# Seven block products in place of eight in the FFN input matrices, with the output matrices in depth parts

## The chip, the cores and the metric

The kernel runs on one core of a Trainium2 chip. The metric is its time on the device in microseconds (us). Engines are called PE (TensorE), DVE (VectorE), ACT (ScalarE), POOL (GpSimd) and SP (SyncE, which issues most DMAs here).

## What is computed

One step of a hybrid encoder of two layers, on 512 prompt tokens and 32 sample tokens with their caches, all in float32. The mixers (attention beside a gated recurrence in layer 0, a delta rule in layer 1) are not touched by the change. Around each mixer stand two half-step FFNs, four in all:

```python
def swiglu(h, w_in, w_out):
    gate, up = jnp.split(h @ w_in, 2, axis=-1)
    return (jax.nn.silu(gate) * up) @ w_out
...
for layer in range(DEPTH):
    x = x + 0.5 * swiglu(rms_norm(x, ffn1_norm[layer]), ffn1_w_in[layer], ffn1_w_out[layer])
    h = rms_norm(x, mix_norm[layer])
    ...
    x = x + o
    x = x + 0.5 * swiglu(rms_norm(x, ffn2_norm[layer]), ffn2_w_in[layer], ffn2_w_out[layer])
```

`w_in` is 1024 x 5632 (2816 gate columns, then 2816 up columns), `w_out` is 2816 x 1024.

## The kernel before

The 544 tokens lie along the free axis, the features on the 128 partitions, so `x` is 8 tiles of 128 x 544. A weight matrix is read in units of 1024 rows by 256 columns (1 MB): SP loads them alternately into `raw[0]` and `raw[1]`. Every operand is split into a rounded high half and the rest: ACT copies `raw` to `wh` (`split_hi`, L553), DVE subtracts to get `wl` (`split_lo`, L558), and PE adds three products, high by high, high by low, low by high (`mm3`, L573). The tokens go in two parts of 288 and 256 columns, so a unit is 8 depth tiles x 2 column tiles x 3 x 2 = 96 matmuls. The `x` side is split in the same way into `xh` and `xl`, the hidden layer into `hh` and `hl`.

An FFN first has 22 input units (`ffn_in_*`): a gate unit (s=0, PSUM slots 0 and 1) and an up unit (s=1, slots 2 and 3) for each of 11 pairs. DVE scales the gate by `rstd` (L714), ACT applies Silu (L677), POOL multiplies by `rstd` again (L698), DVE multiplies by the up part (L724), and ACT and DVE split the hidden tile (L685, L727). Then come 12 output units (`out_pe`, three depth parts for each of four column pairs); the parts of a column pair are added in PSUM, and DVE adds the two finished tiles to `x` (L818). 22 + 11 = 33 units' worth of matmuls in all, the last depth part being shorter.

The order on each engine is the order in which these functions are called; engines meet at semaphores. In the input phase most engines run a hardware loop over the pairs. ACT and DVE prepare the next unit's weights while PE works on the present one.

## Time and profile before

| | us |
|---|---|
| median of 3 runs | 2440.68 (2438.52 to 2443.16) |
| the profiled execution, its own time | 2437.53 |
| its span in the trace | 2435.7 |
| PE busy in the span | 2394.6 |
| DVE busy | 1091.7 |
| ACT busy | 786.6 |
| POOL busy | 375.9 |

The span is what the trace covers; the execution's own time is 1.8 us longer. "Busy" is the time in which an engine has at least one instruction under way. PE's matmuls overlap (one takes longer than the distance to the next), so their pace is read from a stretch and its count.

### The profile page before, as it was taken

The numbers are of one execution on the slowest core, as the hardware profiler recorded it, in microseconds if no ns is written. First come the engines' busy times: TensorE is split into PE (matmuls) and PEld (weight loads), VectorE is DVE, ScalarE is ACT, GpSimd is POOL, SyncE is SP. The second block draws the span as 40 slices with busy tenths as digits, with TensorE's granted clock in tenths as the row PEclk, the third lists the DMA queues.
The fourth block names the chain that finished last, engine by engine and source line by source line (L and its number), as shares of the span: only waits on it lengthen the run. The fifth ranks groups of instructions, "written<-read, shape, count | busy, mean of one in ns | idle before, by whom it ended". The sixth has DMA issues, their size and how long they took to land.

```text
span 2435.7 us, 45344 instructions
## 1 busy us (share of the span) xinstructions
PE 2394.6 (98%) x19160; PEld 2344.4 (96%) x19160; DVE 1091.7 (45%) x1405; ACT 786.6 (32%) x1006; POOL 375.9 (15%) x324
## 2 busy tenths in 40 slices
PE   7999999999999999999999999999999999999998
PEld 7999999988989999999999999999999899999998
DVE  5333332556574333322433332488655654333322
ACT  4333322333323222222322222345345543222222
POOL 2101000000142111000111100143033531011000
PEclk9999999999999999999999999999999999999999
DMA  3223223322202222222222222323200012222221
GB/s 127 91 86 99 82 79 103 101 89 83 68 21 93 87 86 86 82 96 84 95 94 86 86 78 96 98 70 87 71 29 1 10 44 87 87 95 92 83 92 54
DMA packets 191213, 193.66 MB, mean 80 GB/s; under 512 B 4811, under 2 KB 188495, under 8 KB 191082
## 3 DMA queue, kind: packets, MB, share of 16 engines
q1 hardware_dynamic: 178286, 181.64, 23.1%
q10 hardware_dynamic: 12162, 8.11, 1.2%
q0 software_dynamic: 640, 2.10, 0.3%
q8 instruction: 97, 1.59, 0.3%
q14 instruction: 28, 0.22, 0.0%
HBM read 185.73 MB, written 6.10 MB: 79 GB/s over the span
## 4 chain that ended last, share of the span: by engine, by line
PE 94%; DVE 4%; issue 1%; ACT 1%; POOL 0%; DMA 0%; ACTq 0%; DVEq 0%
PE ps L573 81%; PE ps L2522 1%; PE ps L2507 1%; PE ps L2653 1%; DVE wl L558 1%; PE ps L2495 1%; PE ps L1092 0%; PE ps L1560 0%; PE ps L1657 0%; PE ps L780 0%; PE ps L2547 0%; PE ps L2541 0%; PE ps L2553 0%; PE ps L2562 0%; PE ps L1708 0%
## 5 line engine op out<-in xcount | busy, mean ns | idle before, releaser
L573 PE MATMUL ps<-xh,wh 128*128 128x288 f32 x3776 | 780.6, 288 | 3.6 <-DVE wl L558 2.8
L573 PE MATMUL ps<-xl,wh 128*128 128x288 f32 x3776 | 778.4, 287 | 0.0
L573 PE MATMUL ps<-xh,wl 128*128 128x288 f32 x3776 | 775.3, 287 | 0.0
L558 DVE TENSOR_TENSOR wl<-raw,wh 128x2048 fp32r<-128x2048 f32 (+1 forms) x173 | 390.7, 2258 | 505.0 <-ACT wh L553 505.0
L573 PEld LDWEIGHTS ps<-xh,wh 128*128 128x128 f32 x3776 | 577.4, 188 | 16.2 <-issue 8.0
L573 PEld LDWEIGHTS ps<-xh,wl 128*128 128x128 f32 x3776 | 578.1, 188 | 0.0
L573 PEld LDWEIGHTS ps<-xl,wh 128*128 128x128 f32 x3776 | 576.2, 188 | 0.0
L553 ACT ACTIVATE wh<-raw 128x2048 fp32r<-128x2048 f32 (+1 forms) x173 | 323.3, 1869 | 324.7 <-PE ps L573 318.8
L573 PE MATMUL ps<-hl,wh 128*128 128x288 f32 (+1 forms) x1408 | 289.9, 287 | 0.0
L573 PE MATMUL ps<-hh,wl 128*128 128x288 f32 (+1 forms) x1408 | 288.7, 286 | 0.0
L573 PE MATMUL ps<-hh,wh 128*128 128x288 f32 (+1 forms) x1408 | 286.7, 285 | 0.0
L698 POOL TENSOR_TENSOR gbuf<-gbuf,rstd 128x544 f32<-128x544 f32 x88 | 119.9, 1365 | 880.7 <-ACT gbuf L677 880.7
L573 PEld LDWEIGHTS ps<-hh,wl 128*128 128x128 f32 x1408 | 215.3, 188 | 0.0
L573 PEld LDWEIGHTS ps<-hh,wh 128*128 128x128 f32 x1408 | 215.0, 188 | 0.0
L573 PEld LDWEIGHTS ps<-hl,wh 128*128 128x128 f32 x1408 | 214.4, 188 | 0.0
L685 ACT ACTIVATE hh<-sq 128x544 f32 (+1 forms) x88 | 58.1, 660 | 389.2 <-DVE sq L724 389.2
L724 DVE TENSOR_TENSOR sq<-ps,gbuf 128x544 f32<-128x544 f32 x88 | 63.7, 724 | 244.0 <-PE ps L573 244.0
L714 DVE TENSOR_TENSOR gbuf<-ps,rstd 128x544 f32<-128x544 f32 x88 | 63.6, 723 | 201.7 <-PE ps L573 200.3
L677 ACT ACTIVATE gbuf<-gbuf 128x544 f32<-128x544 f32 x88 | 57.5, 658 | 283.4 <-DVE gbuf L714 283.2
L610 POOL TENSOR_TENSOR ssq<-ssq,sq 128x544 f32<-128x544 f32 x49 | 69.4, 1416 | 433.1 <-ACT sq L592 432.2
L818 DVE SCALAR_TENSOR_TENSOR x<-ps,x 128x544 f32 (+1 forms) x48 | 34.6, 723 | 111.7 <-PE ps L573 99.3
L589 ACT ACTIVATE xh<-x,cols (+1 forms) x48 | 36.0, 750 | 141.8 <-DVE x L818 128.7
(430 smaller groups left out, 2191.5 us busy)
## 6 DMA issues: line engine op xcount, KB each, us to landing
raw<-ffn_w_in SPq DMA_DIRECT2D x88, 1024.0 KB, 5.1
raw<-ffn_w_out SPq DMA_DIRECT2D x32, 1024.0 KB, 5.1
raw<-odd_w_in SPq DMA_DIRECT2D x16, 1024.0 KB, 5.6
raw<-even_w_in SPq DMA_DIRECT2D x14, 1024.0 KB, 5.0
raw<-ffn_w_out SPq DMA_DIRECT2D x16, 768.0 KB, 4.9
raw<-even_w_out SPq DMA_DIRECT2D x4, 1024.0 KB, 5.3
raw<-odd_w_out SPq DMA_DIRECT2D x4, 1024.0 KB, 5.4
xnat<-x_prompt SPq DMA_DIRECT2D x2, 1024.0 KB, 8.5
```

Of the source, the lines that this page charges most:

```text
L553: nc.scalar.activation(wh[slot][:, 0:kt, :], raw[slot][:, 0:kt, :], ACT.Copy).then_inc(hi_done.sem, 1)
L558: nc.vector.tensor_tensor(wl[slot][:, 0:kt, :], raw[slot][:, 0:kt, :], wh[slot][:, 0:kt, :].bitcast(F32), ALU.subtract).then_inc(lo_done.s ...
L573: ins = nc.tensor.matmul(ps[:, 2 * pe_out + b, PCOLS[b]], w, r[:, rk, TOKENS[b]], start=first and a == 0, stop=last and a == 2)
L589: nc.scalar.activation(tile(xh, m), tile(x, m), ACT.Copy, scale=gain_of(n, m)).then_inc(xh_ready.sem, 1)
L610: nc.gpsimd.tensor_tensor(ssq[:], ssq[:], sq[m % 2][:], ALU.add).then_inc(ssq_done.sem, 1)
L677: nc.scalar.activation(gbuf[c][:], gbuf[c][:], ACT.Silu).then_inc(gate_silu.sem, 1)
L685: nc.scalar.activation(tile(hh, 2 * j + c), sq[c][:], ACT.Copy).then_inc(hh_ready.sem, 1)
L698: nc.gpsimd.tensor_tensor(gbuf[c][:], gbuf[c][:], rstd[:], ALU.mult).then_inc(gate_rstd.sem, 1)
L714: nc.vector.tensor_tensor(two(gbuf[c][:]), halves(c), two(rstd[:]), ALU.mult).then_inc(gate_scaled.sem, 1)
L724: nc.vector.tensor_tensor(two(sq[c][:]), halves(2 + c), two(gbuf[c][:]), ALU.mult).then_inc(h_made.sem, 1)
L818: nc.vector.scalar_tensor_tensor(out=two(tile(x, m)), in0=halves(2 * q + c), scalar=scale, in1=two(tile(x, m)), op0=ALU.mult, op1=ALU.add) ...
L2495: ins = nc.tensor.transpose(bank(g, 2, n, n)[:, h, :], dX[g][0:n, h, 0:n], ident[0:n, 0:n])
```

## The change

The 22 input units of each FFN become one whole unit as before, three "plain" units whose weights are split in four blocks of 512 elements a partition, and 18 "seven" units. A seven unit cuts its 1024 x 256 weights into 2 x 2 blocks (depth halves by column tiles) and the activations into 2 x 2 blocks (depth halves by token halves of 272), and makes 7 block products by Strassen's scheme (Winograd's form) in place of 8. For it POOL makes four sums of weight blocks for every seven unit (`weight_sums`), and DVE, once for each FFN, the normed activations (`bop_normed`), their four sums (`token_sum`) and, with ACT, their halves (`bop`, seven blocks). The products are put together from PSUM by DVE (`u2c`, `u3c` and four results), with one copy by ACT (`m1c`). High and low halves of weight blocks lie in a ring of eight entries of 512 elements (`entry`).

The functions that go (`ffn_in_*`) are printed above. PE's part of a seven unit, and its waits:

```diff
+        for i, o in enumerate(S_ORDER):
+            op = u.op + i
+            pe.wait_ge(op_lo.sem, op_lo.at(op + 1))
+            if u.at == 2 * LEAD_PAIRS:
+                pe.wait_ge(bop_lo.sem, bop_lo.at(7 * f + i + 1))
+            if i == 4:
+                pe.wait_ge(m1_copied.sem, m1_copied.at(u.seven + 1))
+            if i == 5:
+                pe.wait_ge(block_out.sem, block_out.at(outs_before[u.seven] + 1))
+            if i == 6:
+                pe.wait_ge(block_out.sem, block_out.at(outs_before[u.seven] + 3))
+            w_hi, w_lo = entry(op)
+            for k in range(KH):
+                for a, (w, r) in enumerate(((w_hi, 7 + o), (w_hi, o), (w_lo, 7 + o))):
+                    ins = nc.tensor.matmul(ps[:, bank + S_BANK[i], 0:TH], w[:, k, :], bop[:, r, k, :],
+                                           start=i in S_OPEN and k == 0 and a == 0,
+                                           stop=k == KH - 1 and a == 2, skip_group_check=i in S_ADDED)
+            ins.then_inc(op_used.sem, 1)
```

The sources of the seven weight blocks, their splits, and the sums on POOL:

```diff
+    def op_source(u, i):
+
+        if u.kind != "seven":
+            return block_raw(u, *PLAIN_BLOCKS[i], block_nk(u, i))
+        if i in (0, 4, 5):
+            return block_raw(u, *{0: (0, 0), 4: (0, 1), 5: (1, 1)}[i])
+        return sums_of(u)[:, {2: 0, 1: 1, 3: 2, 6: 3}[i], :, :]
...
+    def op_split_lo(dve, u, i):
+        op, nk = u.op + i, block_nk(u, i)
+        hi, lo = entry(op)
+        dve.wait_ge(op_hi.sem, op_hi.at(op + 1))
+        nc.vector.tensor_tensor(lo[:, 0:nk, :], op_source(u, i), hi[:, 0:nk, :].bitcast(F32), ALU.subtract).then_inc(op_lo.sem, 1)
...
+    def weight_sums(pool, u):
+
+        s, slot, out = u.seven, u.raw % 2, sums_of(u)
+        first = u.seven - ffns[u.f][2 * LEAD_PAIRS].seven
+        pool.wait_ge(raw_loaded[slot].sem, raw_loaded[slot].at(8 * (u.raw - slot) + 16))
+        if first in (2, 3):
+            pool.wait_ge(op_used.sem, op_used.at(ffns[u.f][2 * LEAD_PAIRS].op))
+        elif first > 3:
+            back = [v for v in ffns[u.f] if v.kind == "seven" and v.seven == s - 2][0]
+            pool.wait_ge(op_lo.sem, op_lo.at(back.op + 7))
+        nc.gpsimd.tensor_tensor(out[:, 0, :, :], block_raw(u, 1, 0), block_raw(u, 1, 1), ALU.add).then_inc(sum_made.sem, 1)
+        pool.wait_ge(sum_made.sem, sum_made.at(4 * s + 1))
+        nc.gpsimd.tensor_tensor(out[:, 1, :, :], out[:, 0, :, :], block_raw(u, 0, 0), ALU.subtract).then_inc(sum_made.sem, 1)
+        nc.gpsimd.tensor_tensor(out[:, 2, :, :], block_raw(u, 0, 0), block_raw(u, 1, 0), ALU.subtract).then_inc(sum_made.sem, 1)
+        pool.wait_ge(sum_made.sem, sum_made.at(4 * s + 2))
+        nc.gpsimd.tensor_tensor(out[:, 3, :, :], block_raw(u, 0, 1), out[:, 1, :, :], ALU.subtract).then_inc(sum_made.sem, 1)
```

DVE's part. `next_split` makes a split for the next unit; before an output unit there are only four, at places 3 to 6:

```diff
+    def tail_dve(dve, u):
+
+        if u.kind != "seven":
+            return
+        into = gbuf if u.s == 0 else sq
+        dve.wait_ge(op_used.sem, op_used.at(u.op + 7))
+        nc.vector.tensor_tensor(into[0][:, TH:T], u2c[:], ps[:, 4 * u.s + 2, 0:TH], ALU.add).then_inc(block_out.sem, 1)
+        if u.s == 1:
+            dve.wait_ge(block_silu.sem, block_silu.at(3 * (u.seven // 2) + 3))
+            dve.wait_ge(block_out.sem, block_out.at(outs_before[u.seven] + 6))
+            nc.vector.tensor_tensor(sq[0][:, TH:T], sq[0][:, TH:T], gbuf[0][:, TH:T], ALU.mult).then_inc(h_made.sem, 1)
+            hidden_lo(dve, u, 1, 1)
+
+    def late_tail_dve(dve, u):
+
+        if u.kind == "seven" and u.s == 1:
+            hidden_lo(dve, u, 0, 2)
+
+    def ffn_seven_dve(dve, u):
+        before, pair, outs = ffns[u.f][u.at - 1], u.seven // 2, outs_before[u.seven]
+        into = gbuf if u.s == 0 else sq
+        bank = lambda i: ps[:, 4 * u.s + i, 0:TH]
+        tail_dve(dve, before)
+        next_split(dve, op_split_lo, u, 0)
+        late_tail_dve(dve, before)
+        next_split(dve, op_split_lo, u, 1)
+        dve.wait_ge(m1_copied.sem, m1_copied.at(u.seven + 1))
+        dve.wait_ge(op_used.sem, op_used.at(u.op + 2))
+        nc.vector.tensor_tensor(u2c[:], m1c[:], bank(1), ALU.add).then_inc(block_out.sem, 1)
+        next_split(dve, op_split_lo, u, 2)
+        next_split(dve, op_split_lo, u, 3)
+        dve.wait_ge(block_out.sem, block_out.at(outs + 1))
+        dve.wait_ge(op_used.sem, op_used.at(u.op + 4))
+        nc.vector.tensor_tensor(u3c[:], u2c[:], bank(3), ALU.add).then_inc(block_out.sem, 1)
+        dve.wait_ge(block_out.sem, block_out.at(outs + 2))
+        nc.vector.tensor_tensor(into[1][:, TH:T], u3c[:], bank(2), ALU.add).then_inc(block_out.sem, 1)
+        next_split(dve, op_split_lo, u, 4)
+        if u.s == 1:
+            dve.wait_ge(block_silu.sem, block_silu.at(3 * pair + 1))
+            dve.wait_ge(op_used.sem, op_used.at(u.op + 5))
+            nc.vector.tensor_tensor(sq[0][:, 0:TH], bank(0), gbuf[0][:, 0:TH], ALU.mult).then_inc(block_out.sem, 1)
+        next_split(dve, op_split_lo, u, 5)
+        dve.wait_ge(op_used.sem, op_used.at(u.op + 6))
+        nc.vector.tensor_tensor(into[1][:, 0:TH], u3c[:], bank(1), ALU.add).then_inc(block_out.sem, 1)
+        next_split(dve, op_split_lo, u, 6)
+        if u.s == 1:
+            dve.wait_ge(block_silu.sem, block_silu.at(3 * pair + 2))
+            dve.wait_ge(block_out.sem, block_out.at(outs + 5))
+            nc.vector.tensor_tensor(sq[1][:], sq[1][:], gbuf[1][:], ALU.mult).then_inc(h_made.sem, 1)
```

The activations' part on DVE ahead of the first seven unit, and the raw slots on SP:

```diff
+    def bop_normed(dve, f, n, k):
+
+        first = 6 if k < KH else 4
+        nc.vector.scalar_tensor_tensor(out=bopf[:, first:first + 2, k % KH, :], in0=two(x[:, k, :]), scalar=gain(n, k),
+                                       in1=two(rstd[:]), op0=ALU.mult, op1=ALU.mult).then_inc(bop_norm.sem, 1)
...
+        def token_sum(out, a, b, done, needs):
+            dve.wait_ge(bop_norm.sem, bop_norm.at(8 * f + done))
+            if needs:
+                dve.wait_ge(bop_sum.sem, bop_sum.at(4 * f + needs))
+            nc.vector.tensor_tensor(bopf[:, out, :, :], bopf[:, a, :, :], bopf[:, b, :, :], ALU.subtract).then_inc(bop_sum.sem, 1)
...
+        for k in range(KH):
+            bop_normed(dve, f, n, k)
+        op_split_lo(dve, units[2], 0)
+        token_sum(3, 7, 6, 4, 0)
+        op_split_lo(dve, units[2], 1)
+        for k in range(KH, KT):
+            bop_normed(dve, f, n, k)
+        op_split_lo(dve, units[2], 2)
+        token_sum(1, 5, 7, 8, 0)
+        token_sum(2, 5, 3, 8, 1)
+        op_split_lo(dve, units[2], 3)
+        token_sum(0, 4, 2, 8, 3)
+        hidden(0, 0)
+        hidden(0, 1)
+        hidden_lo(dve, units[1], 0, 1)
+        hidden_lo(dve, units[1], 1, 2)
+        for i in range(4):
+            op_split_lo(dve, units[3], i)
         if f == 0:
             lam_dve(dve)
...
+        gate(1, 0)
+        for i in range(4):
+            bop_split_lo(dve, f, i)
+        gate(1, 1)
+        op_split_lo(dve, units[4], 0)
+        bop_split_lo(dve, f, 4)
+        op_split_lo(dve, units[4], 1)
+        bop_split_lo(dve, f, 5)
+        hidden(1, 0)
+        op_split_lo(dve, units[4], 2)
+        bop_split_lo(dve, f, 6)
+        for i in (3, 4, 5, 6):
+            op_split_lo(dve, units[4], i)
+        hidden(1, 1)
+        hidden_lo(dve, units[3], 0, 1)
+        hidden_lo(dve, units[3], 1, 2)
...
+    def raw_free(sp, index):
+
+        if index < 2:
+            return
+        if index - 2 in plain_of:
+            sp.wait_ge(lo_done.sem, lo_done.at(plain_of[index - 2] + 1))
+            return
+        u = by_raw[index - 2]
+        if u.kind == "seven":
+            sp.wait_ge(sum_made.sem, sum_made.at(4 * u.seven + 4))
+            sp.wait_ge(op_lo.sem, op_lo.at(u.op + 6))
         else:
-            with dve.Fori(0, 2) as jj:
```

The output matrix now comes in three parts, each after the input pairs that make its depth (pairs 0 to 3, 4 to 7, 8 to 10), so that `hh` and `hl` hold 8 tiles in place of 22; DVE adds each part to `x` by itself:

```diff
+            m = 2 * q + c
+            dve.wait_ge(op_used.sem, op_used.at(u.op + 2 * c + 2))
+            if p:
+                dve.wait_ge(x_part.sem, x_part.at(16 * f + 8 * (p - 1) + m + 1))
+            nc.vector.scalar_tensor_tensor(out=two(x[:, m, :]), in0=halves(2 * u.s + c), scalar=0.5, in1=two(x[:, m, :]),
+                                           op0=ALU.mult, op1=ALU.add).then_inc((x_part if p < 2 else x_ready).sem, 1)
+            if c == 0 and v and v.kind == "seven":
+                for i in range(4, 7):
+                    op_split_lo(dve, v, i)
```

The loops are written out. The seven units of an FFN stand in groups of two, four and three pairs, between the lead (units 0 to 3) and the output units.

Where the instructions stand. DVE, one pair of the input phase before (the body of its loop; `wl` and `wh` are the halves of the weights, `gbuf` the gate, `sq` the hidden tile, `hl` its low half):

```order
L558 TENSOR_TENSOR wl1_50<-raw1,wh1_49 128x2048
...
L714 TENSOR_TENSOR gbuf0_66<-ps,rstd 128x544
...
L714 TENSOR_TENSOR gbuf1_67<-ps,rstd 128x544
...
L558 TENSOR_TENSOR wl0<-raw0,wh0 128x2048
...
L724 TENSOR_TENSOR sq0<-ps,gbuf0_66 128x544
...
L724 TENSOR_TENSOR sq1<-ps,gbuf1_67 128x544
...
L727 TENSOR_TENSOR hl_65<-sq0,hh_64 128x544
...
L727 TENSOR_TENSOR hl_65<-sq1,hh_64 128x544
```

DVE after the change, inside the second group of the first FFN, first the gate unit (with the tail of the up unit before it), then the up unit:

```order
L1119 TENSOR_TENSOR sq0<-u2c_75,ps 128x272
L1123 TENSOR_TENSOR sq0<-sq0,gbuf0_68 128x272
L887 TENSOR_TENSOR hl_65<-sq1,hh_64 128x544
L766 TENSOR_TENSOR wl1_50<-raw1,wh1_49 128x512
L887 TENSOR_TENSOR hl_65<-sq0,hh_64 128x544
L766 TENSOR_TENSOR wl0<-wsum1_73,wh0 128x512
L1141 TENSOR_TENSOR u2c_75<-m1c_74,ps 128x272
L766 TENSOR_TENSOR wl0<-wsum1_73,wh0 128x512 x2
L1146 TENSOR_TENSOR u3c_76<-u2c_75,ps 128x272
L1148 TENSOR_TENSOR gbuf1_69<-u3c_76,ps 128x272
L766 TENSOR_TENSOR wl0<-raw1,wh0 128x512
L766 TENSOR_TENSOR wl1_50<-raw1,wh1_49 128x512
```

```order
L1119 TENSOR_TENSOR gbuf0_68<-u2c_75,ps 128x272
L766 TENSOR_TENSOR wl1_50<-raw0,wh1_49 128x512
L766 TENSOR_TENSOR wl1_50<-wsum0_72,wh1_49 128x512
L1141 TENSOR_TENSOR u2c_75<-m1c_74,ps 128x272
L766 TENSOR_TENSOR wl0<-wsum0_72,wh0 128x512 x2
L1146 TENSOR_TENSOR u3c_76<-u2c_75,ps 128x272
L1148 TENSOR_TENSOR sq1<-u3c_76,ps 128x272
L766 TENSOR_TENSOR wl0<-raw0,wh0 128x512
L1153 TENSOR_TENSOR sq0<-ps,gbuf0_68 128x272
L766 TENSOR_TENSOR wl0<-raw0,wh0 128x512
L1156 TENSOR_TENSOR sq1<-u3c_76,ps 128x272
```

One subtraction of 2048 elements a unit has become seven of 512, and between them stand five additions of 272 with one operand in `ps`; the product `sq` by `gbuf` of 544 and one of 272 now have both operands in SBUF, and hidden low halves stand among the splits.

POOL before (the loop over the pairs and its end; `ssq` belongs to the next norm), and after:

```order
L698 TENSOR_TENSOR gbuf0_66<-gbuf0_66,rstd 128x544
...
L698 TENSOR_TENSOR gbuf1_67<-gbuf1_67,rstd 128x544
...
L694 COMPARE_AND_BRANCH
L606 COPY ssq_52<-sq0 128x544
```

```order
L954 TENSOR_TENSOR gbuf0_68<-gbuf0_68,rstd 128x544
L954 TENSOR_TENSOR gbuf1_69<-gbuf1_69,rstd 128x544
L972 TENSOR_TENSOR wsum_first0_70<-raw0 128x512
L974 TENSOR_TENSOR wsum_first0_70<-wsum_first0_70,raw0 128x512
L975 TENSOR_TENSOR wsum_first0_70<-raw0 128x512
L977 TENSOR_TENSOR wsum_first0_70<-raw0,wsum_first0_70 128x512
L954 TENSOR_TENSOR gbuf0_68<-gbuf0_68,rstd 128x544
L954 TENSOR_TENSOR gbuf1_69<-gbuf1_69,rstd 128x544
```

Behind the two gate products that each pair had, POOL now has four sums of 512 elements for each seven unit, all with both inputs in SBUF.

DVE in the lead of the first FFN after the change (`bopf` are the normed activations and their sums); before, a single split and the two products of the pair stood here:

```order
L909 SCALAR_TENSOR_TENSOR bopf_67<-x,cols,rstd 128x2x272 x4
L766 TENSOR_TENSOR wl0<-raw0,wh0 128x512
L1006 TENSOR_TENSOR bopf_67<-bopf_67 128x1088
L766 TENSOR_TENSOR wl0<-raw0,wh0 128x512
L909 SCALAR_TENSOR_TENSOR bopf_67<-x,cols,rstd 128x2x272 x4
L766 TENSOR_TENSOR wl0<-raw0,wh0 128x512
L1006 TENSOR_TENSOR bopf_67<-bopf_67 128x1088 x2
L766 TENSOR_TENSOR wl0<-raw0,wh0 128x512
L1006 TENSOR_TENSOR bopf_67<-bopf_67 128x1088
L1000 TENSOR_TENSOR sq0<-ps,gbuf0_68 128x544
```

The last of these rows is the FFN's first hidden product; all the others stand ahead of it.

## Rows read from the trace of the kernel before

**Rows 1.** The page: busy shares of the engines, chain by engine.
```profile
PE 2394.6 (98%) x19160; PEld 2344.4 (96%) x19160; DVE 1091.7 (45%) x1405; ACT 786.6 (32%) x1006; POOL 375.9 (15%) x324
...
PE 94%; DVE 4%; issue 1%; ACT 1%; POOL 0%; DMA 0%; ACTq 0%; DVEq 0%
```

**Rows 2.** The chain in order of time, layer 1's first FFN: start, us, what.
```profile
1166.75 392.49 PE ps L573 x3168
```

**Rows 3.** Stages: one stretch of an FFN, columns as its head says.
```profile
core 0: us, PE busy (x) PEld busy (x) DVE busy (x) ACT busy (x) POOL busy (x), PEclk, DMA share, GB/s
810.00:1040.00 230.00, 230.00 (x1859) 230.00 (x1858) 83.94 (x76) 59.60 (x57) 24.52 (x18) 1.00 0.28 90
```

**Rows 4.** The chain again, output matrix after layer 1's mixer.
```profile
1977.80 6.39 PE ps L2653 x48
...
1985.07 12.12 PE ps L2653 x96
```

**Rows 5.** Groups by form, DVE: busy us, mean ns, idle before.
```profile
L558 DVE TENSOR_TENSOR wl<-raw,wh 128x2048 fp32r<-128x2048 f32 x157 | 362.6, 2309 | 389.0 <-ACT wh L553 389.0
...
L727 DVE TENSOR_TENSOR hl<-sq,hh 128x544 f32 x80 | 57.6, 720 | 15.9 <-ACT hh L685 15.9
...
L596 DVE SCALAR_TENSOR_TENSOR xl<-x,cols,xh x32 | 25.0, 781 | 9.1 <-ACT xh L589 9.1
...
L625 DVE RECIPROCAL rstd<-ssq 128x544 f32<-128x544 f32 x6 | 21.3, 3550 | 8.8 <-ACT ssq L621 8.8
```

**Rows 6.** DVE in order of time in an FFN unit: start, us, instruction.
```profile
910.24 0.72 DVE L724 TENSOR_TENSOR sq<-ps,gbuf 128x544 f32<-128x544 f32 x1 [5.22 <-PE ps L573]
910.88 0.71 DVE L727 TENSOR_TENSOR hl<-sq,hh 128x544 f32 x1
```

**Rows 7.** DVE in order of time, layer 1's mixer, 256 elements.
```profile
1794.00 0.43 DVE L2229 TENSOR_TENSOR s<-ps,s 128x256 f32<-128x256 f32 x1 [0.20 <-PE ps L2084]
1794.34 0.41 DVE L2230 TENSOR_TENSOR s<-ps,s 128x256 f32<-128x256 f32 x1
```

**Rows 8.** DVE in order of time, layer 1's mixer, 512 elements, and POOL then.
```profile
1780.37 0.69 DVE L2396 TENSOR_TENSOR dBl<-dBT,dlev 128x512 f32<-128x512 f32 x1
...
1781.70 1.26 DVE L2396 TENSOR_TENSOR dBl<-dBT,dlev 128x512 f32<-128x512 f32 x1
...
1781.14 1.27 POOL L2365 TENSOR_TENSOR dU<-ident,dBl 128x512 f32<-128x512 f32 x1 [5.86 <-DVE dBl L2396]
```

**Rows 9.** DVE in order of time, layer 1's mixer, beside rows 10.
```profile
1894.84 1.28 DVE L2435 TENSOR_TENSOR dW<-ps,dW 128x512 f32<-128x512 f32 x2
...
1899.68 3.35 DVE L2009 TENSOR_TENSOR db<-db,ort 128x512 f32<-128x512 f32 x2
```

**Rows 10.** POOL in order of time, the same stretch.
```profile
1894.64 1.27 POOL L2373 TENSOR_TENSOR db<-db,egam 128x512 f32<-128x512 f32 x1
...
1898.33 5.83 POOL L2357 TENSOR_TENSOR dBl<-dBT,dlev 128x512 f32<-128x512 f32 x4
```

**Rows 11.** Groups by form, ACT.
```profile
L685 ACT ACTIVATE hh<-sq 128x544 f32 x80 | 52.8, 660 | 358.5 <-DVE sq L724 358.5
...
L2315 ACT ACTIVATE dZ<-ps 128x512 f32<-128x512 f32 x40 | 23.9, 597 | 13.8 <-PE ps L2507 6.9 <-PE ps L2541 6.9
```

**Rows 12.** DMA issues, the last number is us to landing.
```profile
raw<-ffn_w_in SPq DMA_DIRECT2D x88, 1024.0 KB, 5.1
```

**Rows 13.** The page's group of POOL's gate products.
```profile
L698 POOL TENSOR_TENSOR gbuf<-gbuf,rstd 128x544 f32<-128x544 f32 x88 | 119.9, 1365 | 880.7 <-ACT gbuf L677 880.7
```

**Rows 14.** Stages around PE's longest pause inside the kernel, and its waits.
```profile
719.60:723.00 3.40, 0.69 (x8) 0.45 (x5) 3.21 (x6) 2.04 (x4) 0.00 (x0) 1.00 0.00 0
723.00:726.40 3.40, 3.40 (x14) 3.40 (x15) 2.39 (x3) 1.82 (x2) 0.00 (x0) 0.50 0.00 0
...
PE ps L780 <- DVE mixl L1500: 2.7, 1, 2.7
...
PE ps L1560 <- DVE hq L1465: 1.3, 1, 1.3
```

609 lines of the change are left out of this document (429 added, 180 removed).

## The prediction

> **What bounds the kernel now.** I read the page's shares, then the chain that ended last, then the stages. PE is busy 98% of the span and the chain is 94% PE [rows 1]. Inside an FFN the chain is one unbroken piece of 3168 matmuls, 392.49 us, in each of the four [rows 2]: 3168/96 = 33 units, so 11.893 us a unit and 123.9 ns a matmul. Nothing ever makes PE wait there, while DVE is busy 36% of that time, ACT 26%, POOL 11% [rows 3]. Fewer matmuls therefore shorten the kernel until another engine becomes the bound; DVE is the candidate.
>
> **What is removed.** Of the 22 input units of an FFN, four stay (one whole, three in blocks) and 18 become seven products of 4 x 3 matmuls: 84 of 272 columns in place of 96 of 288 and 256. At 123.9 ns a unit falls to 10.41 us, at most 72 x 1.49 = 107 us in all. But an FFN unit sends two matmuls through each stationary block before the operand pair changes; a product changes it after every one, hi, hi, lo. The output matrix after layer 1's mixer already runs so: 48 matmuls of 288 columns took 6.39 us (133.1 ns), the next 96, half of each width, 12.12 us, 126.3 ns at a mean of 272 [rows 4]. I take that: a product is 1.515 us, a seven unit 10.61 us, saving 1.287 x 72 = **92.7 us**. The 48 output units keep their matmuls. The sum is made against the profiled execution: 2437.5 us, span 2435.7, and 3.2 below the median of the three runs.
>
> **What DVE gets.** A low-half split of 512 elements replaces a quarter of one of 2048. A 512-element operation with two SBUF inputs takes 0.69 us undisturbed [rows 8], 544 takes 0.72 [rows 5]; back to back, operations start 0.08 us earlier than the last one ends (544: 0.64 apart, 256 from PSUM: 0.34 apart) [rows 6, 7]. So I charge 0.61 for a split, 0.64 for 544 elements, 0.35 for a PSUM addition of 272, 0.13 more where it needs the one before.
> - Gate unit (s=0): first the tail of the up unit before it, addition 0.48, product 0.42, two hidden low halves 1.28; then u2, u3 and two results, 1.53, between 7 splits, 4.27. The first split waits 0.7 us, since ACT makes the hidden high half (0.66) and then that split's high half (about 0.6) only after the product [rows 11]. 8.7 us.
> - Up unit (s=1): the gate unit's last addition 0.43, u2 to the results 1.53, two products 0.35+0.66, splits 4.27, and 1.5 us waiting for Silu, two high halves and the M1 copy on ACT. 8.7 us.
>
> That is 17.4 us a pair of units against PE's 21.2. The ends for what the trace doesn't show: an addition of 272 costs between 0.34 (256) and 0.64 (544), ten of them a pair; I stay at the near end. ACT comes to about 6.3 us a unit from its rows, no bound.
>
> **What POOL gets, and what that does to DVE.** POOL now makes four sums of 512 elements for each seven unit, 1.27 us each [rows 10]: 5 us of 10.6. The trace shows what happens beside DVE. With one operand in PSUM nothing: two L2435 operations beside running POOL work took 1.28 together [rows 9]. With both in SBUF DVE stood still: L2396 took 0.69 alone and 1.26 when a POOL operation had begun before it [rows 8]; two L2009 took 3.35, 1.68 each, beside POOL's four L2357, which took 5.83 instead of four times 1.27 [rows 9, 10]. They alternate, and each POOL operation costs DVE 1.68-0.61 = 1.07 us. Splits, bop low halves, hidden low halves and two of the products all have both inputs in SBUF.
>
> The Trainium skill ("SBUF — State Buffer", section "Who interferes with whom") speaks against the change here: such a pair of instructions excludes each other for the whole instruction. The row agrees, save that it charges 1.07 us; by the page's whole 1.27, eight sums would cost a pair up to 10.1 us instead of 8.6, some 1 us more a pair after what hides, 24 us over the 24 pairs that have a burst.
>
> The sums come in a burst. Raw slot v+2 is free after split 5 of unit v, its DMA lands 5.1 us later [rows 12], then POOL starts. I laid a pair out, DVE and POOL alternating. Gate unit: the burst begins 2 to 4 us in, at the first splits; with a sum under u2 (0.35) or under u3 and its result (0.83), of 4.3 us between 3.1 and 3.6 are added, 3.6 once the bursts have moved forward. Up unit: the burst begins near split 3; u3 with its result (0.83), the bank 0 product (0.35) and the last result (0.35) hide 1.5, and 2.8 are added. A pair then takes DVE 12.3+11.55 = **23.85 us**. That is above PE's 21.2, and no better than the 23.79 that the pair costs today. PE loses 2.65 us a pair: product 5 waits for u2, product 6 for the result behind u3 (the banks are reused).
>
> Not every pair pays. Units before output units have no burst beside them (output matrices need no sums) and the last one only four splits, so the last pair of each group runs at PE's pace. DVE may also fall behind by 1.5 to 2 us before product 6 notices: in a free run the result behind u3 is ready 6.9 us into a unit and needed at 9.1. Groups of 4, 3 and 2 pairs: three bursts, 3 x 2.65-1.5 = 6.4; two bursts, 2 x 2.65-1.5 = 3.8; the group of 2 follows the lead.
>
> **The lead**, units 0 to 3, is 4 x 11.9 = 48 us of PE, and the two matmuls of the norm's statistics. DVE must add 8 normed tiles (two SBUF inputs, 0.78 [rows 5]), 4 token sums and 7 low halves of 1088 elements (1.2 to 1.3 each, on the line from 720 ns for 544 to 2309 for 2048): 6+5+9 = 20 us, beside 19 splits (11.6), 8 gate and product operations (5.2), 4 hidden low halves (2.6) and the reciprocal 3.55 [rows 5]. That is 43 us; it starts about 9 us in, behind the statistics, and POOL's four gate products (1.36 each [rows 13]) and first four sums block some 6 us more. So DVE is through with `ffn_lead_dve` near 58 us, the first seven unit starts at 49. Its products 3 and 4 wait about 2 us for their split, then product 5 waits for u2, queued behind the lead: I charge **8 us** an FFN for lead and first group (from 3, if POOL's work falls into DVE's waits, to 14).
>
> Output units: DVE adds each depth part to x, 8 x 0.64 us twice more an FFN, with 4 splits in 11.9 us: hidden under PE. The last hidden tile is ready about 2.4 us after the last product and is needed after 24 matmuls, 2.97 us: nothing. Unrolled loops: nothing.
>
> **Clock.** After a pause of 2.71 us of PE the granted clock was 0.50 for 3.4 us, in which 14 matmuls went in place of 28 [rows 14]. The wait behind each lead is of that size: 1.7 us, 4 times 7 us. The pauses of 1 to 1.6 us in the pairs I charge nothing: one of 1.3 us left the clock alone.
>
> **Sum:** 2437.5-92.7+4 x (6.4+3.8+8)+7 = 2437.5-92.7+72.8+7 = 2424.6, with 3.2 for the median **2428 us**, 0.5% faster. What a measurement tells from no change is 0.2%, 4.9 us.
>
> **Rivals.**
> - *POOL's sums hide* (0.27): bursts mostly fall under PSUM additions, DVE's waits for ACT or for PE. For it: a DVE pair is 17.4 us, and 6.5 of it takes no second SBUF operand; with under 3.8 of the 8.6 us added, PE stays the bound. Against: each sum hides only what stands next to it. 2437.5-92.7+4 x 4+3.2 = 2364; at 107 us removed 2350.
> - *Nothing hides* (0.13): every sum costs DVE its 1.07. A pair is 17.4+8.6 = 26.0, 2.2 more than forecast, over 5 burst pairs an FFN and the lead's: 6 x 2.2 x 4 = 52, so 2480, slower. It decides from 24.4 us a pair on, where the 24 burst pairs have eaten what the forecast leaves. For it: L2009 beside POOL, where every operation paid.
> - *The clock halves in the pairs* (0.18): in a burst pair PE stands 1.6 and 1.3 us with one product between. For it: the one drop in the middle of the trace came behind a pause hardly as long as these two together. Against: the next longest pause, 1.3 us [rows 14], left it at 1.00. Product 6 at half clock is 1.5 us longer and DVE waits for it, some 1.2 us over 24 pairs: 2457, slower.
> - *Forecast* (0.42), its own range 2400 to 2452 with the pair between 23 and 24.8 us.
>
> **Numbers.** Faster: 0.27 of the forecast's 0.42, all of the first rival, 0.03 of the clock's: 0.57. Same 0.10. Slower: 0.13, 0.12 of the clock's, 0.08 of the forecast's: 0.33. The range runs from 2358 (half of the first rival's cases below) to 2475.
>
> **What would show it.** Per step: products in runs of 12 matmuls near 1.51 us (1.49 would give 14 us more); L766 splits near 0.69 us in output units and well above 1 us in gate and up units, while L1141 and L1146 keep 0.45; POOL's L972 to L977 at 1.3 to 1.7 us; PE waiting for DVE's u2c and for the result of u3c, mostly in gate units, some 2 to 4 us a burst pair and none in the last pair before output units; a wait of 4 us in the first seven unit of each FFN; clock 0.5 right behind it. Wrong would make me: DVE ahead of PE through the bursts, waits in front of the output units, or DVE additions slowed by POOL too.

## The result and the profile after

The changed kernel takes 2411.46 us (median of four runs, 2407.56 to 2411.91) against 2440.4 before: ratio 0.9877, interval 0.986 to 0.9894, 29 us or 1.2% faster. The forecast was 2428, that is 12.7 us faster: the sign and the range held, the size did not. The profiled execution has a span of 2405.8 us, 29.9 less than before.

The page of the changed kernel, shares and chain, answering to [rows 1], and its groups for the new lines (L766 is the low half of a split, L972 is the first of POOL's four sums):

```profile
PE 2324.8 (97%) x18296; PEld 2266.1 (94%) x18296; DVE 1649.1 (69%) x2481; ACT 1000.9 (42%) x1735; POOL 750.4 (31%) x540
PE 82%; DVE 12%; issue 3%; ACT 2%; POOL 0%; DMA 0%; ACTq 0%; DVEq 0%
...
L766 DVE TENSOR_TENSOR wl<-raw,wh 128x512 fp32r<-128x512 f32 x456 | 355.1, 809 | 52.1 <-ACT wh L760 51.9
L972 POOL TENSOR_TENSOR wsum<-raw 128x512 f32<-128x512 f32 x64 | 93.8, 1465 | 692.6 <-DMA raw<-ffn_w_in 652.8 <-DVE wl L766 39.8
...
L766 DVE TENSOR_TENSOR wl<-wsum,wh 128x512 fp32r<-128x512 f32 x256 | 250.8, 995 | 50.5 <-ACT wh L760 48.8
```

The chain was 94% PE and is 82% PE and 12% DVE now. A split took 0.69 us undisturbed [rows 8] and takes 0.81 from raw blocks and 1.00 from sums on average; a sum takes 1.47 us and more for 1.27 [rows 10]. The waits of PE, the longest sums first:

```profile
PE ps L840 <- DVE gbuf L1148: 19.5, 21, 2.1
PE ps L840 <- DVE wl L766: 12.4, 8, 2.2
...
PE ps L840 <- ACT m1c L1078: 5.2, 4, 2.2
...
PE ps L840 <- DVE u2c L1141: 1.4, 3, 0.6
```

A "burst" is the run of four sums that POOL makes for a coming unit. The next windows are laid along PE's units in the first FFN, group of 4 pairs, and show its four gate units: the first, which PE gets through without a wait, the second and the third, and the last one, which has only the end of an earlier burst.

```profile
core 0: us, PE busy (x) PEld busy (x) DVE busy (x) ACT busy (x) POOL busy (x), PEclk, DMA share, GB/s
178.31:188.90 10.59, 10.59 (x87) 10.59 (x85) 8.17 (x12) 5.54 (x10) 6.51 (x4) 1.00 0.07 22
...
199.49:214.18 14.69, 12.04 (x86) 11.66 (x85) 13.37 (x17) 6.52 (x12) 6.62 (x5) 0.92 0.23 75
...
225.29:236.46 11.17, 10.82 (x86) 10.62 (x85) 10.42 (x15) 5.98 (x11) 6.32 (x4) 1.00 0.29 95
...
247.06:257.68 10.62, 10.62 (x87) 10.62 (x85) 9.87 (x17) 5.90 (x12) 1.86 (x2) 1.00 0.30 101
```

10.59 us for 84 matmuls is 126.1 ns each: the predicted pace to 0.02 us a unit. So the gain is 92.7 us less what PE then waits, and those waits can be read unit by unit, as the length of each unit over 10.6 us (what PE loses at the lower clock is in it):

| us over the four FFNs | forecast | after |
|---|---|---|
| lead and first group | 32 + 7 for the clock | 31.0 |
| groups of 4 pairs | 25.6 | 19.0 |
| groups of 3 pairs | 15.2 | 10.4 |
| together | 79.8 | 60.3 |

The forecast saved 92.7 and gave 79.8 back; the kernel gave 60.3 back. 92.7-60.3 = 32.4, of which 29.9 is seen in the span. Part of the rest is clock ahead of the seven units: in the first FFN's lead the granted clock was 0.50 from 41.1 to 47.9 us (32 matmuls went from 41.2 to 47.9), where the kernel before lost none. Why it gives that much back, and why not 79.8, is what the runs below are for. How a burst looks in order of time (the unit of 14.69 us):

```profile
205.06 1.65 POOL L974 TENSOR_TENSOR wsum<-wsum,raw 128x512 f32<-128x512 f32 x1
205.49 1.78 DVE L766 TENSOR_TENSOR wl<-wsum,wh 128x512 fp32r<-128x512 f32 x1
...
206.68 1.72 POOL L975 TENSOR_TENSOR wsum<-raw 128x512 f32<-128x512 f32 x1
...
207.19 0.42 DVE L1141 TENSOR_TENSOR u2c<-m1c,ps 128x272 f32<-128x272 f32 x1
...
207.54 3.10 DVE L766 TENSOR_TENSOR wl<-wsum,wh 128x512 fp32r<-128x512 f32 x2
...
207.76 0.48 PE L840 MATMUL ps<-bop,wh 128*128 128x272 f32 x2 [0.54 <-DVE u2c L1141]
...
208.37 1.72 POOL L977 TENSOR_TENSOR wsum<-raw,wsum 128x512 f32<-128x512 f32 x1
...
210.56 0.42 DVE L1146 TENSOR_TENSOR u3c<-u2c,ps 128x272 f32<-128x272 f32 x1
211.02 0.44 DVE L1148 TENSOR_TENSOR gbuf<-u3c,ps 128x272 f32<-128x272 f32 x1
...
211.60 0.62 PE L840 MATMUL ps<-bop,wh 128*128 128x272 f32 x2 [2.11 <-DVE gbuf L1148]
```

A sum holds up the split ahead of u2, which takes 1.78 us and ends at 207.27; product 5 has waited 0.54 us for u2. Two more splits take 3.10 us with POOL's operations in turn, u3 and its result come at 210.56 and 211.02, and product 6, which writes over the bank that the result reads, has waited 2.11 us. The additions that read PSUM kept their 0.42 to 0.44 us, as forecast.

### The profile page after: what moved, and what is told of

Read it like the earlier page. It is cut to its first block, busy times and chain, and to the rows that moved or that the text cites. A ratio compares the mean times of both kernels' runs of the same rounds, so it can differ in the third digit from the quotient of the medians.

```text
span 2405.8 us, 44096 instructions
## 1 busy us (share of the span) xinstructions
PE 2324.8 (97%) x18296; PEld 2266.1 (94%) x18296; DVE 1649.1 (69%) x2481; ACT 1000.9 (42%) x1735; POOL 750.4 (31%) x540
## 4 chain that ended last, share of the span: by engine, by line
PE 82%; DVE 12%; issue 3%; ACT 2%; POOL 0%; DMA 0%; ACTq 0%; DVEq 0%
PE ps L775 26%; PE ps L840 24%; PE ps L664 19%; DVE wl L766 5%; PE ps L2984 1%; ACT wh L760 1%; PE ps L2969 1%; PE ps L3115 1%; DVE wl L649 1%; PE ps L2957 1%; DVE bop L903 1%; PE ps L1554 0%; DVE gbuf L1148 0%; DVE u3c L1146 0%; PE ps L2022 0%
## 5 line engine op out<-in xcount | busy, mean ns | idle before, releaser
L840 PE MATMUL ps<-bop,wh 128*128 128x272 f32 x4032 | 779.4, 292 | 38.7 <-DVE gbuf L1148 19.5
L840 PEld LDWEIGHTS ps<-bop,wh 128*128 128x128 f32 x4032 | 642.2, 191 | 47.3 <-DVE wl L766 33.1
L840 PE MATMUL ps<-bop,wl 128*128 128x272 f32 x2016 | 588.8, 292 | 0.0
L766 DVE TENSOR_TENSOR wl<-raw,wh 128x512 fp32r<-128x512 f32 x456 | 355.1, 809 | 52.1 <-ACT wh L760 51.9
L840 PEld LDWEIGHTS ps<-bop,wl 128*128 128x128 f32 x2016 | 384.9, 191 | 0.0
L972 POOL TENSOR_TENSOR wsum<-raw 128x512 f32<-128x512 f32 x64 | 93.8, 1465 | 692.6 <-DMA raw<-ffn_w_in 652.8
L766 DVE TENSOR_TENSOR wl<-wsum,wh 128x512 fp32r<-128x512 f32 x256 | 250.8, 995 | 50.5 <-ACT wh L760 48.8
L664 PE MATMUL ps<-xh,wh 128*128 128x288 f32 x1088 | 233.1, 296 | 3.3 <-DVE wl L649 2.8
L664 PE MATMUL ps<-xl,wh 128*128 128x288 f32 x1088 | 224.8, 288 | 0.0
L664 PE MATMUL ps<-xh,wl 128*128 128x288 f32 x1088 | 224.0, 287 | 0.0
L664 PEld LDWEIGHTS ps<-xh,wh 128*128 128x128 f32 x1088 | 166.9, 189 | 15.4 <-issue 7.4
L664 PEld LDWEIGHTS ps<-xh,wl 128*128 128x128 f32 x1088 | 166.9, 189 | 0.0
L664 PEld LDWEIGHTS ps<-xl,wh 128*128 128x128 f32 x1088 | 166.8, 189 | 0.0
## 6 DMA issues: line engine op xcount, KB each, us to landing
xnat<-x_prompt SPq DMA_DIRECT2D x2, 1024.0 KB, 12.3
```

The source lines that it names most:

```text
L664: ins = nc.tensor.matmul(ps[:, 2 * pe_out + b, PCOLS[b]], w, r[:, rk, TOKENS[b]], start=first and a == 0, stop=last and a == 2)
L766: nc.vector.tensor_tensor(lo[:, 0:nk, :], op_source(u, i), hi[:, 0:nk, :].bitcast(F32), ALU.subtract).then_inc(op_lo.sem, 1)
L840: ins = nc.tensor.matmul(ps[:, bank + S_BANK[i], 0:TH], w[:, k, :], bop[:, r, k, :], start=i in S_OPEN and k == 0 and a == 0, stop=k == KH ...
L972: nc.gpsimd.tensor_tensor(out[:, 0, :, :], block_raw(u, 1, 0), block_raw(u, 1, 1), ALU.add).then_inc(sum_made.sem, 1)
```

## The experiments

Products are numbered from 0, as in the code. "Waits" are the table's sums again: lead and first group, groups of 4, groups of 3. "Contention theory" stands for the forecast's mechanism: PE waits because POOL's sums hold up VectorE's operations with two SBUF inputs.

### The sums taken away

```
-        nc.gpsimd.tensor_tensor(out[:, 0, :, :], block_raw(u, 1, 0), block_raw(u, 1, 1), ALU.add)
+        nc.gpsimd.tensor_tensor(out[:, 0, :, 0:2], block_raw(u, 1, 0)[:, :, 0:2], block_raw(u, 1, 1)[:, :, 0:2], ALU.add)
         (the other three likewise; the splits read raw blocks, and SP waits for one split more)
```

> POOL's four weight sums make 8 of 512 elements each, and the four splits that read them read raw blocks instead; the output is therefore not the reference's. Everything else of the changed kernel stays. Contention theory: DVE's splits fall from 0.81 and 1.00 us to 0.69, a gate unit costs DVE 8.6 to 8.7 us and an up unit no more, so a pair is far under PE's 21.2. The waits of PE in the groups of 4 and 3 pairs, 29.5 us in the four FFNs, go whole, and of the 31 us of the leads some 15 to 20, since the bursts lie beside the low halves of the token operands there: 2411 - 29.5 - 17 = about 2364 us (2355 to 2375). Rival, latency: PE waits because u2, u3 and the banks go DVE, ACT, DVE in turn, sums or not; then the waits stay at 20 us or more in the groups and the time is above 2390.

Measured: 2348.75 us (2346.55 to 2349.88), ratio 0.9623 (0.9607 to 0.9639). Waits 1.1, -0.2, -0.2 us. Every wait is gone, in the leads too, where only 15 to 20 of 31 us were expected to go. The contention theory holds: without the sums, the order of VectorE and ScalarE's operations costs PE 1.1 us in all, nearly all of it in the first lead. The kernel before less the matmuls alone would be 2440.7-92.7 = 2348.0, so this run also confirms that term of the sum to 1 us. DVE's splits and its load, in windows one unit long:

```profile
L764 DVE TENSOR_TENSOR wl<-raw,wh 128x512 fp32r<-128x512 f32 x744 | 500.4, 695 | 157.9 <-ACT wh L758 157.9
...
894.40:905.00 10.60, 10.60 (x86) 10.60 (x86) 7.40 (x14) 5.03 (x9) 1.20 (x4) 1.00 0.31 100
905.00:915.60 10.60, 10.60 (x86) 10.60 (x86) 8.64 (x16) 6.52 (x12) 1.12 (x4) 1.00 0.32 103
```

An up and a gate unit keep DVE busy 7.40+8.64 = 16.04 us without the sums. The same in the changed kernel, from one tail addition to the next (up, gate, up, gate, up):

```profile
189.10:200.91 11.81, 11.81 (x96) 11.81 (x95) 9.37 (x15) 5.03 (x9) 6.74 (x4) 1.00 0.34 112
200.91:214.52 13.61, 10.96 (x77) 10.59 (x76) 11.95 (x16) 6.52 (x12) 6.32 (x4) 0.90 0.20 67
214.52:226.38 11.86, 11.86 (x93) 11.86 (x93) 9.49 (x15) 5.03 (x9) 6.42 (x4) 0.97 0.24 80
226.38:238.18 11.80, 11.45 (x91) 11.25 (x90) 11.05 (x17) 6.48 (x12) 6.61 (x4) 1.00 0.26 87
238.18:249.43 11.25, 11.25 (x91) 11.25 (x90) 9.77 (x16) 4.97 (x10) 6.42 (x4) 1.00 0.48 155
```

9.37+11.95 = 21.3 and 9.49+11.05 = 20.5: the eight sums add 5.3 and 4.5 us a pair.

### More sums

```
+        if grp:      # burst pairs only; also ahead of the third sum
+            nc.gpsimd.tensor_tensor(out[:, 0, :, :], block_raw(u, 1, 0), block_raw(u, 1, 1), ALU.add).then_inc(extra_sum.sem, 1)
+            pool.wait_ge(extra_sum.sem, extra_sum.at(extra[0] + 1))
```

> In the burst pairs (24 in all, six an FFN) POOL makes the first and the third sum of each unit twice: 6 operations a unit instead of 4, so 4 more a pair; the output stays. Contention theory with DVE bound in every burst pair: each costs DVE 1.07 us less what PSUM operations hide, about two thirds as now (5.8 us added of 8.6), so 2.9 us a pair more: 24 x 2.9 = 70 us, 2480 us (2460 to 2510). Rival, only the first burst pair of a group is bound and later ones have room: 11 or 12 groups x 2.9 = 35 us, 2445. Rival, latency: under 10 us.

Measured: 2479.7 us (2476.94 to 2481.59), ratio 1.0154 (1.0137 to 1.0171); waits 45.9, 55.7, 29.9. That is 68 us more for 96 operations, 0.71 us each, and slower than the kernel before: the price is paid in every burst pair, not only in the first of a group. Clock is in this; in two groups of 3 in which the granted clock stayed at 1.00 PE lost 6.6 and 6.7 us against 2.0 in the changed kernel, for eight operations more, 0.58 us each. With six sums a unit there in place of four, the change would have lost.

### VectorE operations added, from PSUM and from SBUF

```
+        if u.s == 0 and u.at + 2 < len(ffns[u.f]) and ffns[u.f][u.at + 2].kind == "seven":
+            for extra in spare:
+                nc.vector.tensor_tensor(extra[:], m1c[:], bank(1), ALU.add)     # second run: m1c[:], m1c[:]
         nc.vector.tensor_tensor(u2c[:], m1c[:], bank(1), ALU.add).then_inc(block_out.sem, 1)
```

> In the gate unit of each of the 24 burst pairs VectorE adds 272 elements from PSUM twice more, ahead of u2, into spare tiles: 0.35 us each, 0.7 a pair; the output stays. What is asked is how a burst pair's excess reaches PE. DVE bound in every burst pair, with a lag that hides about 2.3 us once a group of pairs: the lag is already used up by the sums in the groups of 4 and 3 and in the first group, so all of it arrives: 24 x 0.7 = 17 us, 2428 us (2424 to 2431). Rival: only the first burst pair of a group pays (2 to 4 us there in the trace, 0.4 to 1.2 in the later ones) and the later ones have room: 12 x 0.7 = 8 us, 2420.

Measured: 2414.25 us (2411.95 to 2418.21), ratio 0.9901 (0.9886 to 0.9917); waits 40.7, 18.1, 6.9. Both expectations missed: 48 operations cost 3 us. In the groups of pairs they cost nothing, only the leads lost, 9.7 us. That is not the clock's doing: it never fell in these groups here, and a group of 4 lost 4.4 to 4.8 us, a group of 3 at most 2.0, as groups without a drop do elsewhere (4.3 and 2.0, see below). So I asked whether it is what they read:

> As e5_more_dve, but the two added operations of 272 elements read both inputs from SBUF. In e5_more_dve they read PSUM, and 48 operations of 0.35 us cost nearly nothing (2414 us) where a bound DVE should have shown 17. Theory: there they stood where a sum was running, which they covered; they only moved the wait. With two SBUF inputs they cover nothing and are held themselves: the 17 us that were expected of e5_more_dve come, 2428 us or more (2424 to 2440). Rival: the gate unit has that much room on DVE at this place (it waits for product 2 anyway), whatever the operations read: 2414 again.

Measured: 2450.15 us (2445.58 to 2452.41), ratio 1.004 (1.0026 to 1.0053); waits 38.1, 41.7, 21.3: 36 us slower than with PSUM, and slower than the kernel before. Some of it is clock, most is not: in the two groups of 3 whose clock stayed at 1.00 PE lost 5.0 and 4.4 us, against 2.0 with PSUM, for four added operations. The two groups of the added operations, from SBUF alone and from PSUM:

```profile
L1144 DVE TENSOR_TENSOR spare<-m1c 128x272 f32<-128x272 f32 x48 | 61.0, 1311 | 0.0
```

```profile
L1144 DVE TENSOR_TENSOR spare<-m1c,ps 128x272 f32<-128x272 f32 x48 | 18.6, 428 | 0.0
```

The same 272 elements take 428 ns with an operand in PSUM and 1311 ns without. At this place an operation that reads PSUM is cover for a running sum and thus free. What bounds DVE is its work and the sums that nothing covers, and the two can't be added up apart.

### Sums placed under that cover

```
+        if timed:    # 2, 4, 6 splits ahead of the sums 1, 2, 3; the unit's end ahead of sum 4
+            pool.wait_ge(op_lo.sem, op_lo.at(nxt.op + 2))
         nc.gpsimd.tensor_tensor(out[:, 0, :, :], ...)
```

> Each sum of a burst waits for the DVE split that stands ahead of PSUM work: sum 1 for split 1 (u2 is next), sum 2 for split 3 (u3 and its result), sum 3 for split 5 (last result), sum 4 for the last split in a gate unit, for the hidden tile in an up unit. Same work. Contention theory: of 1.27 us u2 hides 0.4, u3 and its result 0.8, the last result 0.35, the tail and the wait for Silu 0.9 to 1.3; added a pair about 3.6 to 4.2 in place of 5.3 to 6.3, so the excess of 2.3 us a burst pair falls to about 0.5 and the group waits of 29.5 us to under 10: 2390 us (2383 to 2400). Rival, the spread sums come too late: the first split that reads sum 2 waits for it, and the raw slot is released some 6 us later, so that its transfer of 5.1 us ends later too; then 2415 to 2440.

Measured: 2401.21 us (2400.32 to 2406.51), ratio 0.9843 (0.9826 to 0.986); waits 36.0 (and 1.2 more ahead of the first seven unit), 12.6, 6.2. 10 us better, half of what was expected. In the trace a sum starts 0.22 us behind the u2 that was to cover it:

```profile
908.78 0.44 DVE L1153 TENSOR_TENSOR u2c<-m1c,ps 128x272 f32<-128x272 f32 x1
909.00 1.30 POOL L976 TENSOR_TENSOR wsum<-raw 128x512 f32<-128x512 f32 x1 [11.02 <-DVE wl L766]
909.43 2.21 DVE L766 TENSOR_TENSOR wl<-wsum,wh 128x512 fp32r<-128x512 f32 x2 [0.22 <-ACT wh L760]
```

> As e3_timed_sums, but each sum is released one VectorE operation earlier, so that it stands waiting when the split ahead of the PSUM operation ends, instead of starting 0.2 us behind it as the trace of that kernel shows (split over at 908.8, POOL from 909.00); and on ScalarE the first high half of the first seven unit is made before the second gate tile's Silu of pair 1, which saves VectorE a wait of 1.24 us in each lead. Contention theory: 0.2 us more hidden for each of some 8 sums a pair, at most 24 x 1.6 = 38 us, of which only the 18.8 us of waits that are left in the groups can go: 8 to 12 us there, and 4 x 1 us in the leads: 2388 us (2384 to 2394). Rival: released earlier, a sum begins while VectorE waits for ScalarE just before a split, and holds up that split: no better than e3_timed_sums, 2401.

Measured: 2387.33 us (2385.31 to 2389.14), ratio 0.9787 (0.9774 to 0.98); waits 31.0, 6.2, 2.6: 24 us better than the change, as expected. The leads are where they were in the changed kernel, 6 us better than in the run before, which had the old order on ScalarE.

### Smaller sums

```
-        nc.gpsimd.tensor_tensor(out[:, 0, :, :], block_raw(u, 1, 0), block_raw(u, 1, 1), ALU.add).then_inc(sum_made.sem, 1)
+        nc.gpsimd.tensor_tensor(out[:, 0, 0:2, :], block_raw(u, 1, 0)[:, 0:2, :], block_raw(u, 1, 1)[:, 0:2, :], ALU.add)
+        nc.gpsimd.tensor_tensor(out[:, 0, 2:4, :], block_raw(u, 1, 0)[:, 2:4, :], block_raw(u, 1, 1)[:, 2:4, :], ALU.add).then_inc(sum_made.sem, 1)
```

> Each weight sum is made by two POOL operations of 256 elements in place of one of 512; all else as in the changed kernel, the output stays. If an operation of one engine waits for the whole of the other's (they alternate): a POOL piece takes about 0.65 to 0.7 us and costs VectorE 0.5 to 0.55; POOL makes the same elements, so the added time in total stays about the same and the kernel too, within 5 us of 2411; splits beside the bursts then take 1.2 in place of 1.75 us and there are twice as many of them. Rival: the cost goes with the number of POOL operations: 24 x 8 x 0.7 of added time, up to 80 us slower. Rival, elements share the port by turns: no change at all, split times included.

Measured: 2382.37 us (2379.28 to 2384.76), ratio 0.9769 (0.9754 to 0.9784); waits 27.6, 5.0, 1.6. The split times were as expected, the time was not: 29 us better for the same elements. The time by which the splits (all rows of that line) exceed 0.69 us sums to 153 us in the changed kernel and to 118 here (worked out from all rows of the splits).

> Each sum in four POOL operations of 128 elements, not timed. Halves took 28 us off though POOL made the same elements: the time added to VectorE's splits fell from 153 to 118 us. Theory of the held operation: a POOL operation costs a split at most its own remaining length and PSUM operations of 0.44 us hide it; at 0.35 us a piece fits under one of them whole, but pieces and splits still alternate, 16 pieces at 0.69+0.35 make 17 us a burst, longer than a unit of 10.6, and the sums come late for the splits that read them. So the added time falls again, to about 90 us, but some of the gain is lost to late sums: 2375 to 2385 us. Rival, a fixed price an operation: 1152 operations of at least 0.2 us each, 2400 or more.

Measured: 2370.17 us (2369.28 to 2371.99), ratio 0.9715 (0.97 to 0.973); waits 26.7, 0.0, -0.2, excess of the splits 80 us. Better than expected again, and the sums did not come late. DVE and POOL in an up unit's burst:

```profile
910.28 0.89 DVE L766 TENSOR_TENSOR wl<-wsum,wh 128x512 fp32r<-128x512 f32 x1 [0.82 <-ACT wh L760]
910.57 0.91 POOL L975 TENSOR_TENSOR wsum<-raw 128x128 f32<-128x128 f32 x1
...
911.14 0.44 DVE L1158 TENSOR_TENSOR u3c<-u2c,ps 128x272 f32<-128x272 f32 x1
911.56 0.46 POOL L977 TENSOR_TENSOR wsum<-wsum,raw 128x128 f32<-128x128 f32 x1
911.61 0.44 DVE L1160 TENSOR_TENSOR sq<-u3c,ps 128x272 f32<-128x272 f32 x1
911.96 0.68 DVE L766 TENSOR_TENSOR wl<-raw,wh 128x512 fp32r<-128x512 f32 x1
911.98 0.99 POOL L978 TENSOR_TENSOR wsum<-wsum,raw 128x128 f32<-128x128 f32 x1
```

and with halves, a gate unit:

```profile
922.40 1.23 DVE L766 TENSOR_TENSOR wl<-wsum,wh 128x512 fp32r<-128x512 f32 x1
923.55 0.42 DVE L1145 TENSOR_TENSOR u2c<-m1c,ps 128x272 f32<-128x272 f32 x1
923.90 2.02 DVE L766 TENSOR_TENSOR wl<-wsum,wh 128x512 fp32r<-128x512 f32 x2
```

A split that is held takes 1.78 us beside a whole sum, 1.23 beside a half and 0.89 to 0.97 beside a quarter, so a piece costs 1.09, 0.54 or 0.2 to 0.28: for a whole sum's elements about the same. What changes, by these rows, is how many pieces are held against: the quarter at 911.56 runs whole under u3's result of 0.44, and the split behind it takes its 0.68. A whole sum of 1.3 us is longer than such an operation and reaches past it. POOL pays in turn: its next quarter, held by the split, takes 0.99 us.

### The lead

```
-            nc.vector.tensor_tensor(bopf[:, out, :, :], bopf[:, a, :, :], bopf[:, b, :, :], ALU.subtract)
+            nc.vector.tensor_tensor(bopf[:, out, :, 0:2], bopf[:, a, :, 0:2], bopf[:, b, :, 0:2], ALU.subtract)
```

> The four token sums of 1088 elements on VectorE make 8 elements each (2 columns of 4 tiles), and the operands made from them are split from a normed tile; the output is not the reference's. The lead theory of the prediction: DVE works through the lead without a rest and ends late by what it has too much, so 5 us less of work on it takes up to 5 us of the 7 to 8 us that PE loses in each lead and first group: about 4 x 4 to 5 = 16 to 20 us, 2393 us (2390 to 2397). Rival, the wait of the first seven unit is set by the order behind the second gate tile of pair 1 (low halves, splits, POOL's second burst), not by the sum of the work: under 4 us, 2409.

Measured: 2395.58 us (2393.41 to 2397.17), ratio 0.9814 (0.9798 to 0.9831); waits 17.7, 17.3, 11.1. 16 us off for 20 us less work, 13 of them in the leads: less work on VectorE reaches PE there, as the forecast had it. Then two attempts to mend its order, each on top of smaller sums:

```
+        if u.at == 2 * LEAD_PAIRS:      # behind the M1 copy, and likewise the low half behind u2
+            hidden_hi(act, ffns[u.f][3], 1, 2)
```

> Everything that the runs so far spoke for, together: sums in halves of 256 elements (2382 us alone), each pair of halves released ahead of the PSUM operations (2387 us with the Silu order in the lead), and in the lead the second hidden tile of pair 1 is made behind the M1 copy, since product 4 of the first seven unit waits up to 4.0 us for that copy in the run with halves. Contention theory: the waits in the groups fall from 6.6 us to about 2, those of the leads from 27.6 to 12 to 18 us (1.2 us for ScalarE's order, 2 us for the copy, in each of four): 2382 - 4 - 12 = 2366 us (2360 to 2373). Rival: the lead is bound by the sum of DVE's work and not by the order, so only what the order of the halves hides goes: 2378 to 2382.

Measured: 2375.91 us (2371.88 to 2376.68), ratio 0.9732 (0.9719 to 0.9746); waits 29.9, -0.2, -0.2. The groups gave all they had, the leads nothing. The time lies between the expectation and its rival.

```
-        weight_sums(pool, ffns[f][4])
-        gate(1, 0)
-        gate(1, 1)
+        weight_sums(pool, ffns[f][4], gate)      # gate(1, 0) behind sum 2, gate(1, 1) behind sum 3
```

> Quarter sums as in e10_quarter_sums, which left no wait in the groups and 26.5 us in the four leads, and four changes of order in the lead: ScalarE makes the first high half of the first seven unit ahead of the second gate tile's Silu of pair 1 (VectorE stood 1.25 us for it); POOL makes its two gate products of pair 1 behind the second and third sum instead of behind the fourth (VectorE stood 1.68 us for the first of them, and both ran only at 797 us); VectorE makes the second hidden tile of pair 1 behind split 4 instead of 6, so that ScalarE's M1 copy, queued behind it, comes earlier (product 4 waited up to 3.0 us for that copy). If VectorE's standing time is what is left: 2.9 us less in each lead and some of the copy's wait, 10 to 16 us in all: 2357 us (2353 to 2361). Rival, seen in e9_half_timed, where a similar move only changed the name of the wait: VectorE's work in the lead is the bound, the gate products now hold it up earlier instead: 2365 to 2371.

Measured: 2374.64 us (2370.58 to 2377.22), ratio 0.9729 (0.9716 to 0.9742); waits 27.6, -0.1, -0.2. That is 4 us slower than quarters alone, past the rival's 2371 too: the leads gained nothing (27.6 against 26.7). What PE waits for in the first seven unit, first with quarters alone, then with the new order:

```profile
PE ps L840 <- ACT m1c L1090: 12.1, 4, 3.0
```

```profile
PE ps L840 <- DVE u2c L1157: 11.9, 4, 3.1
```

The wait has a new name and the same size.

### The order of a product's matmuls

```
-                for a, (w, r) in enumerate(((w_hi, 7 + o), (w_hi, o), (w_lo, 7 + o))):
+                for a, (w, r) in enumerate(((w_hi, 7 + o), (w_lo, 7 + o), (w_hi, o))):
```

> In every block of a seven product the matmuls go high x high, low x high, high x low instead of high x high, high x low, low x high: now neighbours share the moving operand, not the stationary one; the output stays but for rounding. The prediction's step is that a product runs at 126.1 ns a matmul because the operand pair changes after each one. By it nothing changes: 126 ns, 2411 us. Rival: the 2.2 ns over the 123.9 of the other FFN units come from the order of the operands; then the pace falls to 124 ns and the time by up to 72 x 84 x 2.2 ns = 13 us.

Measured: 2416.45 us in one run; an undisturbed unit still takes 10.59 to 10.60 us. The pace does not hang on which operand neighbours share. Where the 2.2 ns over the other FFN units come from stays open.

## Why the prediction was right and wrong

- **The matmuls, 92.7 us:** right (10.59 against 10.61 us a unit; 2348.75 us where nothing waits).
- **VectorE's own work:** 16.0 us busy a pair without sums; the forecast's 17.4 with 2.2 of waiting in it was 15.2 busy, 0.8 short.
- **What a sum costs, 1.07 us held against a split:** right, 1.78-0.69 = 1.09. By the Trainium skill ("SBUF — State Buffer", "Who interferes with whom"), which excludes for the whole instruction, it would be 1.3, that length; the trace shows 0.2 less. The runs from PSUM and SBUF agree with its rule on which operations are held.
- **What the eight sums add to a pair, 3.6+2.8 = 6.4 us:** too much, 4.5 to 5.3 us of busy time measured: 3.3 and 2.4 in two gate units, 2.0 and 2.1 in two up units.
- **The pair at 23.85 us:** right, by luck. Two units with the clock at 1.00, the up unit from 189.10 and the gate unit from 226.38, take VectorE 11.81+11.80 = 23.6 us. Only 20.4 of that is busy, against 21.6 forecast, and 3.2 is waiting, against 2.2: two errors of 1 us cancel.
- **The lag that hides, 1.5 us a group:** right. VectorE's last addition of a unit starts 0.2 us behind PE's end where nothing is late and 1.8 to 1.9 us behind it in the last burst unit of two groups of 3 and of one of 4 (run without token sums) where the clock did not fall, 1.6 to 1.7 more. In the group shown, behind a drop, 2.2 were hidden: VectorE's five units from 189.10 to 249.43 take 7.3 us more than PE's 53.0, and PE ended the fifth, at 247.06, 5.2 us late.
- **This is the step that failed:** "PE loses 2.65 us a pair", charged for three whole pairs less 1.5 (6.4) and two whole pairs less 1.5 (3.8). Measured, 4.7 and 2.6, which is 11.4 us less over four FFNs; where the clock did not fall, 4.3 (the second FFN of the run without token sums, the same code in its groups) and 2.0 (the third and fourth FFN). The first gate unit of a group stands behind an output unit and has no up unit's tail in it: of the 12.3 us that the forecast gave a gate unit, 2.9 are that tail and the wait behind it, and what is left is under PE's 10.6. The trace bears it out. VectorE is busy 8.17 us in that unit (the window from 178.31), with its burst in it, and ends it 0.2 us behind PE:

```profile
178.51 0.72 DVE L1179 SCALAR_TENSOR_TENSOR x<-ps,x 128x544 f32<-128x544 f32 x1 [1.56 <-PE ps L775]
179.24 0.69 DVE L766 TENSOR_TENSOR wl<-raw,wh 128x512 fp32r<-128x512 f32 x1
180.97 0.69 DVE L766 TENSOR_TENSOR wl<-wsum,wh 128x512 fp32r<-128x512 f32 x1 [1.04 <-ACT wh L760]
181.60 0.44 DVE L1141 TENSOR_TENSOR u2c<-m1c,ps 128x272 f32<-128x272 f32 x1
```

  So five units pay 1.2 us each in a group of 4, and three in a group of 3: 6.0-1.7 = 4.3 and 3.6-1.6 = 2.0, the values measured. By the forecast's own prices the first unit was 1.7 us of the charge of each of the eight groups, 14 us in all. This is worked out from the order and the trace; no run changes it alone. The first FFN pays 1.1 us more in each of its two groups: in the second gate unit the first sum starts 0.04 or 0.02 us ahead of the second hidden low half and holds it to 1.83 or 1.86 us; in the other FFNs it starts 0.02 to 0.21 us behind, and the low half takes its 0.72.
- **The second term that failed, 7 us for the clock behind the leads:** it was added to the lead's wait, and cost nothing. The granted clock fell to 0.50 in three of the four first seven units, and from the start of product 2 to the start of product 4 all four take 5.83 us: product 4 waits for the M1 copy in any case, 2.25 us where the clock stayed and 0.94 to 1.03 us where it fell. The two steps (11.4 and 7) and 1 us of the lead are the 19.5 us between 79.8 and 60.3. What makes PE wait was as forecast; what was wrong is for how many units it was charged, and a price charged twice. And since a charge of 80 was taken from a saving of 93, a quarter off the charge doubled the gain.
- **Where the waits stand:** in gate units, as forecast, but unevenly: in the group shown the second gate unit loses 4.1 us and the later ones 0.6 and 0.0. The last pair of a group loses nothing but for one wait of 1.2 us, in the third FFN's group of 4.
- **The lead, 8 us:** 7.7. Product 1 waits 0.3 to 1.5 us for its split and product 2 waits 2.2; product 4 waits 0.9 to 2.2 us for ScalarE's M1 copy, which the forecast did not name; products 3 and 5, which it did, wait for nothing, and product 6 waits 0.3.
- **The clock:** the forecast was four drops behind the leads. The granted clock was 0.50 for 3.4 us eight times among the seven units: three in leads, five in the pairs, each behind a wait:

```profile
208.20:211.60 3.40, 1.29 (x11) 1.10 (x10) 3.37 (x5) 0.66 (x2) 1.89 (x2) 1.00 0.00 0
211.60:215.00 3.40, 3.40 (x16) 3.40 (x17) 2.45 (x5) 0.66 (x2) 0.00 (x0) 0.53 0.31 92
```

  In the pairs a drop costs 1.5 us in the two units behind it (a group of 3 loses 3.5 us with it at the same wait of 1.8 us, 2.0 without). In a group of 4 the third gate unit then waits for less, 0.6 to 0.8 us in place of 2.4, so that the group loses 4.3 to 4.5 us with a drop in the second and fourth FFN and 4.3 without one. So the clock rival came true in 5 of 24 burst pairs, and cost at most 7 us (five times 1.5, less what the third gate units gave back), not 29. In the run with no waits the clock fell nowhere among the seven units.
- **The rivals:** "POOL's sums hide" did not happen, though quarter sums made it so (its 2364 against 2370). "Nothing hides" wanted 8.6 us added to a pair where 4.5 to 5.3 were, and it would have made the added operations from PSUM cost their whole time.

## What to carry to other kernels

Where GpSimd and VectorE both read SBUF, count VectorE's time per operation as its own plus what is left of GpSimd's operation when it starts, and look at what each stands next to. Cut GpSimd's operations to the size of VectorE's PSUM operations, or release them just ahead of these: quarter sums alone made this change worth 70 us (2370.17, ratio 0.9715) instead of 29, at no cost in VectorE's work; whole sums released early, 52 us; halves released early, 64 us. Quarters released early were not run. When a price per unit is multiplied by a number of units, look at what stands ahead of the first and behind the last of them, and add a clock charge to a wait only if nothing else ends that wait later. And where a forecast is one large number less another, the smaller one's error decides the size of the gain: price it as a range.

## What the hardware showed beyond that

- Smaller pieces cost GpSimd more time and the kernel less. A quarter took 0.46 us alone, four 1.8 against 1.3 for the whole, and all were made in time.
- 48 added VectorE operations cost 3 us in all with an operand in PSUM, none of it in the groups, and 36 us more with both in SBUF (0.43 against 1.31 us each).
- The granted clock fell to 0.50 behind PE's pauses of 0.54 and 2.11 us at 208 to 212 us, and stayed at 1.00 through pauses of 0.57 and 2.09 us at 345 to 349 us, at the same place of the next group, and through pauses of 2.19 and 2.25 us, some 4 us apart, behind the first lead. What tells them apart, no run here shows.
- Not tried: a lead of three pairs. It would put two plain units, 23.8 us, more ahead of the first seven unit for 2.6 us of matmuls an FFN; the first sums' buffers lie where its hidden tiles would go.
